# State products of a gated-DeltaNet head in four groups, p5 copied by ScalarE, z emptied one bank at a time, and the head loop 6 KB further in TensorE's program

## The reference, cut to what matters

```
proj = h @ w_in                         # q, k (16 heads), v (32 heads), gate z, beta, a
qkv, conv_new = causal_conv(qkv, ...)   # 4 taps, then SiLU
q, k = l2norm(q) * dk**-0.5, l2norm(k); beta = sigmoid(..); g = -exp(a_log) * softplus(..)
# per chunk: L = (beta k) k^T * decay (strictly lower); T = (I + L)^-1
u = T v*beta - (T (beta k exp(gc))) S
o = (q exp(gc)) S + ((q k^T) * decay) u
S = S * exp(g_last) + (k exp(g_last - gc))^T u
out = (rmsnorm(o) * silu(z)) @ w_out
```

## Time and profile before

| what | value |
|---|---|
| median of 3 runs | 2135.55 us (2132.77 to 2158.35) |
| profiled execution, its own time | 2137.08 us |
| its span | 2135.4 us |
| TensorE busy (share of the span) | 2073.1 us (97%) |
| VectorE busy | 1317.4 us (62%) |
| ScalarE busy | 842.4 us (39%) |
| GpSimd busy | 252.1 us (12%) |
| chain that ended last, by engine | PE 90%, DVE 5%, issue 3%, ACT 1% |
| loop of the 15 passes | 111.45 to 1069.40 us |
| a pass | 62.6 us in ten of them |

### The profile page before, as it was taken

How to read it: one execution, slowest core, us unless ns; L and a number is a source line. 1 busy time by engine, 2 the same in 40 slices (tenths; PEclk the granted TensorE clock), 3 DMA queues, 4 the chain that set the end, 5 groups by cost and what they waited for, 6 DMA issues and landing times.

```text
span 2135.4 us, 51389 instructions
## 1 busy us (share of the span) xinstructions
PE 2073.1 (97%) x19533; PEld 1980.2 (93%) x19533; DVE 1317.4 (62%) x2203; ACT 842.4 (39%) x1674; POOL 252.1 (12%) x354
## 2 busy tenths in 40 slices
PE   6999999999999999999999999999999999999998
PEld 4889998989999999998889999999999999999997
DVE  4567777666777677677755444555555556654443
ACT  3444443434444434444443333433333333333333
POOL 3022121121121222112110010000000000000010
PEclk9999999999999999999999999999999999999999
DMA  5545544455453455545356445544444454444442
GB/s 162 148 117 148 148 141 129 118 149 148 133 163 113 134 163 146 153 132 150 117 156 192 138 143 173 158 146 149 159 154 146 155 162 156 146 152 150 157 140 88
DMA packets 379995, 311.40 MB, mean 146 GB/s; under 512 B 19609, under 2 KB 375866, under 8 KB 379322
## 3 DMA queue, kind: packets, MB, share of 16 engines
q1 hardware_dynamic: 378042, 306.30, 47.5%
q10 hardware_dynamic: 1872, 3.96, 0.5%
HBM read 283.85 MB, written 27.25 MB: 146 GB/s over the span
## 4 chain that ended last, share of the span: by engine, by line
PE 90%; DVE 5%; issue 3%; ACT 1%; DMA 0%; DVEq 0%; SPq 0%; ACTq 0%
PE ps L296 27%; PE ps L298 25%; PE ps L297 25%; PE ps L1153 8%; PE ps L1317 1%; DVE wlo L287 1%; DVE dec L946 1%; DVE convout L937 1%; PE ps L1174 1%; DMA xtok<-in_x_sample_dram 0%; ACT zraw L635 0%; DVE sq L843 0%; PE ps L1223 0%; PE ps L1267 0%; DVE s_s L1086 0%
## 5 line engine op out<-in xcount | busy, mean ns | idle before, releaser
L296 PE MATMUL ps<-xhi,whi 128*128 128x320 f32 x3072 | 995.1, 324 | 16.9 <-ACT zraw L635 7.4
L298 PE MATMUL ps<-xhi,wlo 128*128 128x320 f32 x3072 | 954.6, 311 | 2.3 <-issue 2.3
L297 PE MATMUL ps<-xlo,whi 128*128 128x320 f32 x3072 | 954.2, 311 | 2.7 <-issue 2.7
L287 DVE TENSOR_TENSOR wlo<-wraw,whi 128x1024 fp32r<-128x1024 f32 (+1 forms) x484 | 615.6, 1293 | 230.7 <-ACT whi L282 228.0
L296 PEld LDWEIGHTS ps<-xhi,whi 128*128 128x128 f32 x3072 | 581.4, 189 | 41.0 <-issue 32.9
L282 ACT ACTIVATE whi<-wraw 128x1024 fp32r<-128x1024 f32 (+1 forms) x484 | 495.6, 1049 | 262.6 <-PE ps L298 236.7
L298 PEld LDWEIGHTS ps<-xhi,wlo 128*128 128x128 f32 x3072 | 580.6, 189 | 6.0 <-issue 6.0
L297 PEld LDWEIGHTS ps<-xlo,whi 128*128 128x128 f32 x3072 | 581.8, 189 | 0.8
L298 PE MATMUL ps<-bhi,wlo 128*128 128x320 f32 x512 | 158.2, 309 | 0.0
L297 PE MATMUL ps<-blo,whi 128*128 128x320 f32 x512 | 158.2, 309 | 0.0
L296 PE MATMUL ps<-bhi,whi 128*128 128x320 f32 x512 | 158.1, 309 | 0.0
(11 more groups left out here) (338 smaller groups left out, 2171.9 us busy)
## 6 DMA issues: line engine op xcount, KB each, us to landing
wraw<-in_delta_w_in_dram SPq DMA_DIRECT2D x384, 256.0 KB, 3.2
wraw<-in_pool_w_in_dram SPq DMA_DIRECT2D x256, 256.0 KB, 3.1
wraw<-in_delta_w_out_dram SPq DMA_DIRECT2D x128, 256.0 KB, 3.3
wraw<-in_pool_w_out_dram SPq DMA_DIRECT2D x128, 256.0 KB, 3.2
s_s<-in_state_delta_dram SPq DMA_DIRECT2D x32, 512.0 KB, 6.3
out_dram<-s_s SPq DMA_DIRECT2D x32, 512.0 KB, 5.0
wraw<-in_pool_w_group_dram SPq DMA_DIRECT2D x64, 256.0 KB, 3.1
dec<-gc_rows SPq DMA_DIRECT2D x16, 320.0 KB, 5.0
```

The lines of the kernel that those rows point to most:

```text
L287: nc.vector.tensor_tensor(wlo[:, slot, 0:width], wraw[:, slot, 0:width], whi[:, slot, 0:width].bitcast(F32), ALU.subtract).then_inc(E("w_l ...
L296: mm(o, whi[:, slot, w], hi[:, k_x, :], start=first, stop=False)
L297: mm(o, whi[:, slot, w], lo[:, k_x, :], start=False, stop=False)
L298: done = mm(o, wlo[:, slot, w], hi[:, k_x, :], start=False, stop=last)
```

## The change

- **States.** The 32 state products are cut into four groups of eight (`states_part`), each right behind lxt of levels 1 to 4, in the place of a fill of one piece. The fills ahead of lxt grow from 2, 1, 2, 3, 2 to 3, 3, 3, 4, 2 pieces, and the one behind the qkv transposes shrinks from 8 to 7, so that a pass still has 48 pieces. `ksqs_ps` is signalled after the fourth group. r4 and o4 move behind the levels on VectorE. On GpSimd the scaling of `s_s` moves behind ym.
- **p5** is copied by ScalarE instead of VectorE; split 8 of ScalarE follows it. The decay exponents of the next head stand behind the transpose of level 4.
- **v** is emptied behind y5 and `cc_tail` stands behind p6.
- **z.** In the last two k steps of z the products are ordered by output tile, all six of h = 0 before those of h = 1; `z_half` is signalled in between, and ScalarE empties bank 0 on it and bank 1 on `w_used`. For head 0 it now stands ahead of `samp`.
- **Loop moved.** 25 products with one column each at the start of TensorE's program.

```diff
-    def k_tile(slot, k_w, hi, lo, k_x, pair, first, last):
+    def k_tile(slot, k_w, hi, lo, k_x, pair, first, last, halves=(0, 1)):
 
         mm = nc.tensor.matmul
-        for h in range(2):
+        for h in halves:
...
             next_hidden()
-            pool.wait_ge(E("ksqs_ps"), n)
-            sv = s_s[:].rearrange("p b v c -> p (b v) c")
-            gp.tensor_tensor(sv, sv, wide(cur[:, EGL + 4:EGL + 20], 16), ALU.mult).then_inc(E("s_scaled"), 1)
             pool.wait_ge(E("y4"), n)
             gp.tensor_tensor(ym[:].rearrange("p u (q c) -> p u q c", q=4), yc[:].rearrange("p u (o c) -> p u o c", o=1).to_broadcast(
                 [P, 5, 4, BL]), blocks4[:].rearrange("p (o q) c -> p o q c", o=1).to_broadcast([P, 5, 4, BL]), ALU.mult
                              ).then_inc(E("ym"), 1)
+            pool.wait_ge(E("ksqs_ps"), n)
+            sv = s_s[:].rearrange("p b v c -> p (b v) c")
+            gp.tensor_tensor(sv, sv, wide(cur[:, EGL + 4:EGL + 20], 16), ALU.mult).then_inc(E("s_scaled"), 1)
...
         def z_evac(i, used):
-            act.wait_ge(E("w_used"), used)
+            act.wait_ge(E("z_half"), i + 1)
             if loop_of(i):
                 act.wait_ge(E("gate"), i)
-            sc.activation(zraw[:], ps[:, 0:2, 0:T], ACT.Copy).then_inc(E("z_evac"), 1)
+            sc.activation(zraw[:, 0, :], ps[:, 0, 0:T], ACT.Copy)
+            act.wait_ge(E("w_used"), used)
+            sc.activation(zraw[:, 1, :], ps[:, 1, 0:T], ACT.Copy).then_inc(E("z_evac"), 1)
...
-            if loop_of(i):
-                z_evac(i, i * 12 + (HEADS + 12))
+            z_evac(i, i * 12 + (HEADS + 12))
...
                 units = 5 if k < S_LEVELS else 4
+                if k == TILE_LEVELS:
+                    act.wait_ge(E("lp5"), n)
+                    sc.activation(p5[:], blocks(D0[:, 0:P], 4), ACT.Copy).then_inc(E("p5"), 1)
+                    split(8)
                 act.wait_ge(E("lxt"), (n - 1) * 5 + k)
...
-                if k < 5:
+                if k < 4:
                     split(4 + k)
+            v_next()
             act.wait_ge(E("lp6"), n)
             sc.activation(p6[0:64, :, :], blocks(D0[0:64, 0:256], 4), ACT.Copy).then_inc(E("p6"), 1)
+            tail_next()
             split(9)
...
                 else:
-                    v.tensor_copy(p5[:], blocks(D0[:, 0:P], 4)).then_inc(E("p5"), 1)
                     dve.wait_ge(E("x4"), n)
...
-                if k == 3:
-
-                    dve.wait_ge(E("ksqs_ps"), n)
-                    dve.wait_ge(E("rqe"), n)
-                    v.scalar_tensor_tensor(vb[:, 4, :], D3[:, 256:384], cur[:, NBE + 4:NBE + 5], vb[:, 4, :], ALU.mult, ALU.add
-                                           ).then_inc(E("r4"), 1)
-                    v.tensor_scalar(o_m[:, 4, :], D3[:, 384:512], small[:, 20:21], None, ALU.mult).then_inc(E("o4"), 1)
-                if k == 4:
-                    decays_next()
                 if k < TILE_LEVELS:
...
                     if k == TILE_LEVELS - 1:
                         turned.then_inc(E("x4"), 1)
+                        decays_next()
...
+            dve.wait_ge(E("ksqs_ps"), n)
+            dve.wait_ge(E("rqe"), n)
+            v.scalar_tensor_tensor(vb[:, 4, :], D3[:, 256:384], cur[:, NBE + 4:NBE + 5], vb[:, 4, :], ALU.mult, ALU.add
+                                   ).then_inc(E("r4"), 1)
+            v.tensor_scalar(o_m[:, 4, :], D3[:, 384:512], small[:, 20:21], None, ALU.mult).then_inc(E("o4"), 1)
             conv_next(1, 0)
...
+        for w in range(25):
+            one(ps[:, 3, w:w + 1], ident[:], ident[:, w:w + 1])
         pe.wait_ge(E("x_in"), 48)
...
-                last = k_tile((p // PK) % 4, k % PK, xhi, xlo, k, job % 2, k == 0, k == KT - 1)
+                slot = (p // PK) % 4
+                if job < 2 or k < KT - 2:
+                    last = k_tile(slot, k % PK, xhi, xlo, k, job % 2, k == 0, k == KT - 1)
+                elif k == KT - 1:
+                    for h in range(2):
+                        for kk in (KT - 2, KT - 1):
+                            last = k_tile(slot, kk % PK, xhi, xlo, kk, job % 2, False, kk == KT - 1, (h,))
+                        if h == 0:
+                            last.then_inc(E("z_half"), 1)
...
-            fill(8)
+            fill(7)
...
+            def states_part(part):
+
+                if part == 0:
+                    pe.wait_ge(E("kq_m"), n)
+                    pe.wait_ge(E("state_landed"), n * 32)
+                m, b0 = part // 2, 2 * (part % 2)
+                for b in range(b0, b0 + 2):
+                    for j in range(4):
+                        h, q = j % 2, j // 2
+                        at = (2 * m + h) * P + 32 * b
+                        last = mm(D3[32 * j:32 * j + 32, 256 + P * m:384 + P * m], kq_m[:, at:at + 32],
+                                  s_s[:, 4 * h + b, q, :], start=b == 0, stop=b == 3)
+                if part == 3:
+                    last.then_inc(E("ksqs_ps"), 1)
...
-                fill((2, 1, 2, 3, 2)[k - 1])
-                if k == 2:
...
+                fill((3, 3, 3, 4, 2)[k - 1])
                 x = x0 if k == 1 else xc
                 pe.wait_ge(E("ident"), 1)
+                if k == TILE_LEVELS:
+                    pe.wait_ge(E("x4"), n)
...
                 if k < TILE_LEVELS:
-                    fill(1)
+                    states_part(k - 1)
```

More of the change, by code:

```diff
@@ L690, in branch_hi, with delta @@
             sc.activation(xhi[:, 4 * ch:4 * ch + 4, :], branch[:, 4 * ch:4 * ch + 4, :], ACT.Copy).then_inc(E("b_hi"), 1)
-        def delta(n, split, cached, store, next_silus, begun):
+        def delta(n, split, cached, store, next_silus, begun, v_next, tail_next):
             begun()
@@ L778, in delta_act @@
         silus(0)
-        z_evac(0, HEADS + 12)
         act.wait_ge(E("t_exp"), 1)
@@ L787, in split @@
                     qk_evac(i, i * 12 + (HEADS + 4))
[L788 to L792, removed]
+            delta(i, split, lambda i=i: cc_evac(i), lambda i=i: cc_store(i), lambda i=i: silus(i), lambda: None,
+                  lambda i=i: v_evac(i, i * 12 + (HEADS + 8)), lambda i=i: cc_tail(i))
         def out_split(j):
@@ L802, in delta_act @@
         branch_hi(0)
-        delta(NH, out_split, lambda: None, lambda: None, lambda: None, out_begun)
+        delta(NH, out_split, lambda: None, lambda: None, lambda: None, out_begun, lambda: None, lambda: None)
     def delta_dve(dve):
@@ L1010, in delta @@
                 units = 5 if k < S_LEVELS else 4
-                dve.wait_ge(E("c_all"), 1)
-                dve.wait_ge(E(f"lp{k}"), n)
                 if k < TILE_LEVELS:
+                    dve.wait_ge(E("c_all"), 1)
+                    dve.wait_ge(E(f"lp{k}"), n)
                     v.copy_predicated(half_blocks(pc[:, k - 1, 0:units, :], k, 1),
@@ L1307, in delta @@
                 last.then_inc(E(f"lp{k}"), 1)
-                fill((2, 1, 2, 3, 2)[k - 1])
-                if k == 2:
-                    pe.wait_ge(E("kq_m"), n)
-                    pe.wait_ge(E("state_landed"), n * 32)
-                    for m in range(2):
-                        for b in range(4):
-                            for j in range(4):
-                                h, q = j % 2, j // 2
-                                at = (2 * m + h) * P + 32 * b
-                                last = mm(D3[32 * j:32 * j + 32, 256 + P * m:384 + P * m], kq_m[:, at:at + 32],
-                                          s_s[:, 4 * h + b, q, :], start=b == 0, stop=b == 3)
-                    last.then_inc(E("ksqs_ps"), 1)
+                fill((3, 3, 3, 4, 2)[k - 1])
                 x = x0 if k == 1 else xc
                 pe.wait_ge(E("ident"), 1)
+                if k == TILE_LEVELS:
+                    pe.wait_ge(E("x4"), n)
                 pe.wait_ge(E(f"p{k}"), n)
```

## The result

The changed kernel takes 2166.05 us, median of 5 runs (2164.13 to 2168.59), beside 2135.86 us for the kernel before on the same chip (5 runs, 2132.77 to 2158.35). The ratio is 1.0111, with an interval of 1.0064 to 1.0158: slower by about 1%, less than 2%. The profiled executions took 2168.59 and 2137.1 us, 31.5 apart, and all of it lies in the loop: from the first product of the loop to the first behind it were 957.95 us before (111.45 to 1069.40) and are 989.42 us now.

A forecast was written before the change was run, and what follows sets the result against it. Weight products were taken to fill TensorE, busy for 61.80 of a 62.63 us pass. Savings of 4.5, 4, 7 and 1 against costs of 37.5 and 15 gave +36 on 2137.1, 2173; it said 2168, range 2110 to 2188.

The forecast's parts named there:

- the wait for x5: TensorE before xt6: GpSimd's moved scaling holds VectorE, x5 comes late; 2.5 us in 15 passes, +37.5 (0 to +45).
- the clock: TensorE falls to half clock behind the x5 wait, three times in four, 1.3 us each: +15 (0 to +22).
- the 25 products: Small products at the start of TensorE's program run while TensorE waits for x: 0 (-1 to +2).
- the fetches: Loop's new place against fetched instruction blocks: from -12.7 (whole loop stays) to +50 (fetch every pass); taken as 0.
- the groups: State products in four groups on TensorE: four blocks' entries saved, two tile changes per group paid; -1 (-13 to +5).
- Rival 1: No wait for x5: GpSimd's scaling lets VectorE through or starts late enough; 2120, with fetches gone 2108; chance 0.22.
- rival 2: Slower by over 2%: same wait, TensorE at half clock in every pass; 2184, deciding from 4.0 us per pass; chance 0.2.
- p5 by ScalarE: ScalarE copies p5 instead of VectorE, so TensorE's 7.0 us of waits for it go: -7.0 (-7.5 to -5).
- z bank by bank: Half of z is emptied under the last six products, each pass starts 0.27 us earlier: -4.0 (-5 to 0).
- rival 4: The groups save what the blocks cost, changes between small products being free: 2156; held in the forecast's chance of 0.53.
- Rival 3: The loop fetches its instruction blocks each pass: some 4 us per pass, +50, 2170 to 2220; chance 0.05.
- The first emptying of z: Before the loop, z emptied ahead of samp removes TensorE's wait (-3.2) and low clock (-1.3): -4.5 (-5 to 0).

The follow-up runs named there:

- decays_late: Changed kernel with the five decay exponents of the next head behind the first part of o on VectorE, not behind the transpose of level 4: 2120.46 us, ratio 0.9886.
- old_states: Changed kernel with all 32 state products in one group at level 2, the old fills, and GpSimd's scaling ahead of ym again: 2105.87 us, ratio 0.984.
- before_z: Kernel before with only z emptied bank by bank and, for the first head, ahead of samp: 2130.98 us, ratio 0.9927.
- before_shift: Kernel before with only the 25 small products added at the start: 2124.78 us, ratio 0.9891.
- no_shift: Changed kernel without the 25 small products at the start: 2190.59 us, ratio 1.0235.
- scale_after_x5: Changed kernel with one more wait, so that GpSimd scales the states only when x5 is written: 2132.39 us, one run.

## Why the prediction came out right

The main cause was foreseen: the wait for x5, with its chain and its length. That the number, 2168 beside 2166.05, came so close is luck. Four terms were off and cancelled: the clock by 13 us and the 25 products by 4 too low, the fetches by 13 and the groups by 4 to 5 too high. The sum itself gave 2173; the step from there to 2168 is the 1.5 us that the profiled execution lies above the median, and for the rest part of the fetches going, which the same sum put at 0.

The sum as the runs show it, for the 31.5 us between the two profiled executions: the quiet pass is 62.63 - 61.37 = 1.26 shorter, 15 times -18.9; the waits for x5 15 x 2.39 = +35.9; the low clock behind them +28.4 (from wait to wait there are 65.38 us eleven times and 66.75 three times; less 61.37 and 2.39 that leaves 1.62 and 2.99, and the fifteenth I take as 1.6); the fetches of the loop -12.7; the start -3.8 and +3.75; and some -1.2 left over for the first pass and the last wait. Together +31.4.

- **The wait for x5, predicted 2.5 us in 15 passes: right, 2.39,** but for the last pass, where I had none and 0.97 came. The chain was as described: ym, one exponent through, scaling, then four exponents, two copies, a split and the copy from PSUM. x5 is there 8.1 us after the end of y4 (412.54 to 420.65), predicted 8.2 to 8.4. Rival 1 is out; of what I set down for it, that "the copies and the turn are not held", only the turn holds (0.30 inside the scaling): in decays_late a copy of xm took 3.56, and in the last pass of the kernel after 2.45. By the Trainium skill, SBUF — State Buffer, Who interferes with whom, copies and multiplications by a scalar may enter modes that take the ports shared with GpSimd, an instruction with two inputs in SBUF contends with a GpSimd instruction that reads SBUF, and whoever issues first keeps the ports for the whole instruction. The runs agree, with 3.70 for an exponent, 3.56 for a copy and 3.71 for two multiplications.
- **The clock behind it, predicted +15: about half of what came, 28.** I took a drop in three passes of four at 1.3 us; there was one in every pass, of 1.6, and in every fourth of 3.0. This is the mechanism of rival 2 (a drop in every pass), without its sum: 2.39 + 1.9 is 4.3 per pass, above the 4.0 from which I had it decide, but the savings were larger too.
- **p5 by ScalarE, -7.0, and z bank by bank, -4.0: close.** z gave 0.21 a pass where I had 0.27. p5, with the moves of v, the tails, r4 and o4, was measured only as what is left: 1.26 less 0.21 and 0.35 to 0.41 is 0.64 to 0.70, and old_states beside before_z gives 0.69, where the wait was 0.50 to 0.56. Some 0.1 us a pass is in none of my steps, and no run takes it apart.
- **Four groups, -1: wrong, -5 to -6.** The step failed in pricing both changes of kind of a group at 0.11. Only the one from states to Y costs (0.11 to 0.14); rival 4 had it half right. The rule of TensorEngine Tiling (Array Packing), Key Properties, in the Trainium skill, that a change of mode drains TensorE, is seen in one direction here and not in the other.
- **The fetches, 0 in the sum: wrong, -12.7 in the profiled pair; before_shift gives -20 on the median of its chip, with the later start already in it.** I named both ends, and no row of before could tell; before_shift does. Rival 3 (a fetch in each pass) is out: behind the first pass there is none.
- **The first emptying of z, -4.5: right in kind.** The wait fell from 3.46 to 0.49; from the gates' first product to the loop's first are 65.15 us instead of 68.98. It doesn't show in the place of the loop, 111.37 after 111.45, because of the next term.
- **The 25 products, start 0: wrong, +3.75 in this pair.** "They run while TensorE waits for x" holds for the first 9 us only; they outlast the wait by 2 us, and TensorE runs slowly longer behind them (a transpose takes 0.42 us until about 29 us, before until 23.5, and 0.27 from there on). Over all profiled executions, the gates' first product comes at 44.6 on average in the eight kernels with the products at the head, at 41.1 in the three without them.

## What to carry to other kernels

Before a GpSimd instruction over SBUF is moved, list what VectorE issues next at the new place and who waits for that: in this kernel every exponent, copy, multiplication by a scalar and split that came second, all from SBUF to SBUF, sat until the scaling of 3.6 us was done; only the transpose didn't. So a move that gains 0.4 us a pass lost 4. If no place is free, cut the work into short pieces on an engine that isn't held, as ScalarE's 16 instructions of 0.39 us here. And a loop whose time differs by tens of us from run to run may be fetching its own instructions: look at that queue's packets, and try the loop a few dummy instructions further on, put into a wait that is long enough.

## What the runs showed of the hardware

- A stall of fetching belongs to the place of a loop and to chance together. The kernel before lay between 2127.19 and 2175.19 us in all its runs, and in its profiled execution two turns of the loop behind the first pass fetched nine packets each (from one xt6 to the next pass 70.09 us there, and 67.91, instead of 62.63). With the 25 products ahead of it none did in the profiled execution, and 10 runs lay between 2123.15 and 2127.63 us. Why the same program fetches in one execution and not in the next stays open.
- The clock fell behind each wait of 2.39 us, 15 in the kernel after and 15 in no_shift. Behind the waits of 1.12 us in decays_late it fell once in 15, and behind those of 1.75 in scale_after_x5 never in 15: the quiet passes, 62.54 and 63.40, hold little beside the 61.4 us of work and the wait. So the length of the wait alone doesn't decide it. The drop is long in every fourth pass, in no_shift too, with the same wait before it; I have no cause for that.
- Beside GpSimd's scaling of 3.6 us, VectorE's instructions from SBUF to SBUF took 3.40 (multiplication), 3.55 (split), 3.56 (copy) and 3.70 us (exponent). Its transpose (0.30), a predicated copy from PSUM (0.23) and an addition with one operand in PSUM (0.82) ran inside the scaling at their usual length.
- How long the start runs slowly differs between executions: with the same 25 products at the head, the granted clock is recorded as full from 21.2 us on in decays_late and from 29.4 in the kernel after. The kernels with these products at the head had the gates' first product at 42.53 to 46.22, the others at 40.27 to 42.47.
